# Sums of squares behind two feed-forward parts: ones times squares on TensorE between the half tiles, in place of GpSimd's adds

## The chip, the cores and the metric

The kernel runs on one core of a Trainium2 chip. The metric is device time in microseconds of one execution, taken as the median of several runs.

## The reference, cut to what matters

A model of four layers on 512 tokens of width 1024, in fp32. The change lies behind the two gated feed-forward parts of the first two layers, where this is computed (g are gain vectors, f is the feed-forward result):

```python
f = conv_glu_ffn(rms_norm(x, ffn_pre_g[layer]), ...)      # 1024 -> 2 x 2816 -> 1024
x = x + rms_norm(f, ffn_post_g[layer])                    # "m": statistic over f
# behind layer 0:
hkv = rms_norm(x, kv_norm_g); kv = hkv @ w_kv             # "x": statistic over the new x
h = rms_norm(x, mix_pre_g[1]); q = h @ w_q
# behind layer 1 (second model):
h = rmsnorm(x, norm_mix_g[0]) * (1 + sc1) + sh1
u = h @ s5_w_in                                           # then the S5 recurrence
```

So between the last product of a feed-forward part and the first product of what follows there are two RMS norms, one after the other: mean of f squared, rstd, x updated, mean of x squared, rstd, x scaled.

## The kernel before, in words

Activations lie transposed: a chunk c (0 to 7) is 128 channels on the partitions by 512 tokens. Every weight product is done in three fp32r matmuls (L470 hi by hi, L471 lo activation, L472 lo weight). For that ScalarE writes the high part of a weight tile (`split_hi`, L1114) and VectorE the low part (`split_lo`, L1843), one tile ahead of TensorE, and each normalised chunk is split in the same way (ScalarE `split_halves`, L1173; VectorE L1913 or L1915 in `norm_half`). All engines run their own instruction streams in written order and meet at semaphores; a wait at the head of a stream holds all that stands behind it.

At the two places of the change the work is cut into halves h of 256 tokens, so that half 0's norms can run beside half 1's products. I write "tile 0" and "tile 1" for the last two weight tiles of the output product (`out_pair`: tile 0 half 0, tile 1 half 0, tile 0 half 1, tile 1 half 1; 11 chunks of 3 matmuls, 33 in each), which make chunks 6 and 7 of f. Then comes the first product of the next part: behind the first feed-forward part a key tile and a value tile for half 0 (48 matmuls each), then half 1; behind the second one the two tiles of the S5 input product, also 48 each and half 0 first. A dictionary of hooks, keyed (tile, half, chunk), says at which chunk TensorE stops between its products to do something for a norm.

The norms of one half before: ScalarE squares a chunk (L1147) into one of two buffers, GpSimd adds it to sqsum (L2791), TensorE multiplies sqsum by a column of ones (`norm_sum`, L574: tokens come to lie on partitions), ScalarE takes the root (`norm_std`, L1156), VectorE the reciprocal (L1888), TensorE spreads it over all partitions (`norm_spread`, L581), and VectorE uses it: L1930 and L1934 update x chunk by chunk (`post_halves`), L1908 scales x (`norm_half`). I call the statistics m0, x0, m1, x1: of f or of the new x, for half 0 or 1.

At the start of the program the same norms are already done in another way: each squared chunk is a matmul with a full 128 x 128 matrix of ones (L589, `start_sum`), summed in PSUM. A root over one row of 256 tokens (L1280) and two matmuls with a one-column output (L598) bring it back to partitions, and the reciprocal is L2059.

The order on VectorE before, behind a feed-forward part: x of half 0 (eight chunks, with f of half 1 in between), low part of weight tile A, three chunks of half 1's x, then `norm_half(0)`, low part of weight tile B, five chunks of half 1's x, `norm_half(1)`. Tile B is the value tile, or the second S5 input tile.

## Time and profile before

| | |
|---|---|
| median of 3 runs | 2524.06 us (2520.86 to 2525.45) |
| the profiled execution: its own time | 2525.14 us |
| its span in the trace | 2523.3 us |
| TensorE busy | 94% of the span |
| VectorE, ScalarE, GpSimd busy | 57%, 42%, 18% |
| chain that ended last | TensorE 76%, VectorE 13%, ScalarE 5% |

The time is the span and 1.8 us around it. The places of the change lie at 414 to 482 us and at 1080 to 1140 us of the span. Rows of the timeline give the start, the duration, and in brackets how long the engine had been idle and who released it. Matmuls overlap in the pipeline, so a matmul's cost in a stream is the distance between starts, not its duration.

### The profile page before, as it was taken

The numbers are of one execution on the slowest core, as the hardware profiler recorded it, in microseconds if no ns is written. First come the engines' busy times: TensorE is split into PE (matmuls) and PEld (weight loads), VectorE is DVE, ScalarE is ACT, GpSimd is POOL, SyncE is SP. The second block draws the span as 40 slices with busy tenths as digits, with TensorE's granted clock in tenths as the row PEclk, the third lists the DMA queues.
The fourth block names the chain that finished last, engine by engine and source line by source line (L and its number), as shares of the span: only waits on it lengthen the run. The fifth ranks groups of instructions, "written<-read, shape, count | busy, mean of one in ns | idle before, by whom it ended". The sixth has DMA issues, their size and how long they took to land.

```text
span 2523.3 us, 34462 instructions
## 1 busy us (share of the span) xinstructions
PE 2368.9 (94%) x12994; PEld 1990.8 (79%) x12994; DVE 1429.5 (57%) x1988; ACT 1064.6 (42%) x1545; POOL 455.3 (18%) x408
## 2 busy tenths in 40 slices
PE   9999998888899999879798999999999999999998
PEld 8788877767788788667588888888877778988887
DVE  5675677857477757668735423336656642542433
ACT  5553543435545334543344313325446652431331
POOL 0230232322333223135410000011002201000001
PEclk9999999899899999979899999999999999999999
DMA  5345552212235455343121222222211202222221
GB/s 199 136 181 178 182 178 95 94 61 88 89 122 189 160 176 188 136 161 139 70 100 68 100 100 97 87 79 99 103 52 36 70 34 101 84 100 99 86 98 67
DMA packets 56346, 282.49 MB, mean 112 GB/s; under 512 B 7996, under 2 KB 19008, under 8 KB 28336
## 3 DMA queue, kind: packets, MB, share of 16 engines
q1 hardware_dynamic: 34144, 213.84, 23.6%
q0 software_dynamic: 12560, 58.80, 6.7%
q10 hardware_dynamic: 9536, 8.39, 1.0%
q8 instruction: 72, 1.18, 0.2%
q14 instruction: 34, 0.28, 0.0%
HBM read 265.14 MB, written 15.86 MB: 111 GB/s over the span
## 4 chain that ended last, share of the span: by engine, by line
PE 76%; DVE 13%; ACT 5%; issue 3%; POOL 2%; DMA 0%; ACTq 0%; DVEq 0%; SPq 0%; POOLq 0%
PE ps L470 22%; PE ps L471 21%; PE ps L472 21%; DVE w_lo L1843 3%; ACT w_hi L1114 2%; PE ps L1017 1%; PE ps L1018 1%; PE ps L1019 1%; POOL gl L2863 1%; DVE tg L1908 1%; DVE v L2484 1%; PE ps L1051 1%; POOL sqsum L2791 1%; DVE ada_w L1851 1%; PE ps L790 1%
## 5 line engine op out<-in xcount | busy, mean ns | idle before, releaser
L470 PE MATMUL ps<-h_hi,w_hi 128*128 128x512 f32 (+1 forms) x2016 | 743.3, 369 | 35.0 <-DVE w_lo L1843 21.1
L471 PE MATMUL ps<-h_lo,w_hi 128*128 128x512 f32 (+1 forms) x2016 | 732.6, 363 | 0.0
L472 PE MATMUL ps<-h_hi,w_lo 128*128 128x512 f32 (+1 forms) x2016 | 732.0, 363 | 0.0
L1843 DVE TENSOR_TENSOR w_lo<-raw,w_hi 128x2048 fp32r<-128x2048 f32 x193 | 442.1, 2291 | 463.1 <-ACT w_hi L1114 462.9
L1114 ACT ACTIVATE w_hi<-raw 128x2048 fp32r<-128x2048 f32 x193 | 369.0, 1912 | 391.5 <-PE ps L472 389.2
L470 PEld LDWEIGHTS ps<-h_hi,w_hi 128*128 128x128 f32 x2016 | 387.7, 192 | 102.0 <-issue 19.7
L470 PE MATMUL ps<-a_hi,w_hi 128*128 128x512 f32 (+1 forms) x1164 | 428.6, 368 | 30.4 <-DVE f L2300 13.7
L471 PEld LDWEIGHTS ps<-h_lo,w_hi 128*128 128x128 f32 x2016 | 388.2, 193 | 57.7 <-issue 1.0
L472 PEld LDWEIGHTS ps<-h_hi,w_lo 128*128 128x128 f32 x2016 | 388.1, 192 | 57.5
L471 PE MATMUL ps<-a_lo,w_hi 128*128 128x512 f32 (+1 forms) x1164 | 424.9, 365 | 0.0
L472 PE MATMUL ps<-a_hi,w_lo 128*128 128x512 f32 (+1 forms) x1164 | 424.8, 365 | 0.0
L2791 POOL TENSOR_TENSOR sqsum<-sqsum,sq 128x256 f32<-128x256 f32 (+1 forms) x124 | 122.7, 990 | 1029.2 <-issue 604.8
L470 PEld LDWEIGHTS ps<-a_hi,w_hi 128*128 128x128 f32 x1164 | 223.8, 192 | 70.1 <-DVE a_lo L2287 9.3
L472 PEld LDWEIGHTS ps<-a_hi,w_lo 128*128 128x128 f32 x1164 | 223.7, 192 | 34.2
L471 PEld LDWEIGHTS ps<-a_lo,w_hi 128*128 128x128 f32 x1164 | 224.1, 193 | 33.7
L2863 POOL TENSOR_TENSOR gl<-gl,tv 128x512 f32<-128x512 f32 x44 | 119.7, 2721 | 220.0 <-ACT gl L1350 220.0
L1147 ACT ACTIVATE sq<-x 128x256 f32<-128x256 f32 (+1 forms) x88 | 41.3, 475 | 240.1 <-DVE x L2556 96.1
L1851 DVE SCALAR_TENSOR_TENSOR ada_w<-ada_w,cond 128x1024 f32<-128x1024 f32 x96 | 113.4, 1218 | 0.0
L2278 DVE SCALAR_TENSOR_TENSOR tg<-ps,vec,tg 128x511 f32<-128x511 f32 x88 | 65.5, 744 | 42.8 <-ACT tg L1345 40.3
L1352 ACT ACTIVATE a_hi<-gl 128x512 f32 (+1 forms) x44 | 27.8, 632 | 132.9 <-POOL gl L2863 132.9
L2287 DVE TENSOR_TENSOR a_lo<-gl,a_hi 128x512 f32 (+1 forms) x44 | 30.5, 692 | 90.5 <-ACT a_hi L1352 90.5
L2836 POOL DMA_DIRECT2D ada_w<-ada_dram x47 | 27.6, 587 | 252.9 <-DVE ada_w L1851 247.5
(397 smaller groups left out, 2716.3 us busy)
## 6 DMA issues: line engine op xcount, KB each, us to landing
raw<-weights_dram SPq DMA_DIRECT2D x161, 1024.0 KB, 4.8
ada_w<-ada_dram POOLq DMA_DIRECT2D x48, 1024.0 KB, 5.1
raw<-weights_dram SPq DMA_DIRECT2D x32, 704.0 KB, 4.0
par<-par_dram SPq DMA_DIRECT2D x8, 1152.0 KB, 7.9
par_dram<-plane POOLq DMA_DIRECT2D x10, 512.0 KB, 3.9
tab<-tab_dram SPq DMA_DIRECT2D x8, 512.0 KB, 5.7
x_tok<-x_rows_dram SPq DMA_DIRECT2D x4, 512.0 KB, 5.8
x<-x_in_dram SPq DMA_DIRECT2D x1, 2048.0 KB, 14.2
```

The costliest lines, as they stand in the source:

```text
L470: nc.tensor.matmul(dst, w_hi[:, o:o + P], rhs_hi, start=start, stop=False)
L471: nc.tensor.matmul(dst, w_hi[:, o:o + P], rhs_lo, start=False, stop=False)
L472: return nc.tensor.matmul(dst, w_lo[:, o:o + P], rhs_hi, start=False, stop=last)
L1114: nc.scalar.activation(w_hi[:, u * TILE:(u + 1) * TILE], raw[:, u * TILE:(u + 1) * TILE], ACT.Copy).then_inc(w_hi_done, 1)
L1147: nc.scalar.activation(dst, src, ACT.Square, **scaled).then_inc(sq_ready, 1)
L1352: nc.scalar.activation(chunk(a_hi, slot.now()), chunk(gl, u), ACT.Copy).then_inc(a_hi_done, 1)
L1843: nc.vector.tensor_tensor(w_lo[:, o], raw[:, o], w_hi[:, o].bitcast(f32), SUB).then_inc(w_split, 1)
L1851: ins = nc.vector.scalar_tensor_tensor(w, w, 1.0, cond[:, :], MUL, MUL, accum_out=mod_at[:, m:m + 1])
L2278: ins = nc.vector.scalar_tensor_tensor(t[:, u * T + s:(u + 1) * T], ps[:, (2 * u + m) * T:(2 * u + m) * T + T - s], v("conv_w", j + (wcol ...
L2287: nc.vector.tensor_tensor(chunk(a_lo, slot.now()), chunk(gl, u), chunk(a_hi, slot.now()).bitcast(f32), SUB).then_inc(a_ready, 1)
L2791: gp.tensor_tensor(dst, dst, src, ADD).then_inc(sq_added, 1)
L2863: gp.tensor_tensor(chunk(gl, u), chunk(gl, u), chunk(tv, u), MUL).then_inc(prod_done, 1)
```

## The change

Behind both feed-forward parts the statistics are summed as at the start: ScalarE squares a half chunk into one of four slots of sq, and TensorE multiplies it by the matrix of ones into a bank of PSUM. GpSimd still adds the first six chunks of f, which come as whole tiles; TensorE takes its two halves in as one product each (`pooled_sum`). The roots, columns and reciprocals are those of the start. The hooks put these products between the chunks of the half tiles. On ScalarE and VectorE the order is changed too. "f" names the place behind the first feed-forward part, "g" the one behind the second. The helpers of the start are renamed and shared (`start_sum` is `square_sum`, `start_col` is `std_column`, `start_rstd` is `rstd_column`), with one list of slots for all squares; the start does the same work in the same order.

TensorE:

```diff
+        def square_sum(name):
+
+            norm, c = name[:-1], int(name[-1])
+            b0, col = SUM_AT[norm]
+            pe.wait_ge(sem("start_act"), STEP[name])
+            s = SLOT[name]
+            nc.tensor.matmul(bank(b0, TH, off=col), ones[:, :], sq[:, s * TH:(s + 1) * TH], start=(c == 0), stop=(c == DC - 1)).then_inc(sem("start_pe"), 1)
+
+        def pooled_sum(p, h):
+
+            pe.wait_ge(sq_added, POOLED[p])
+            b0, col = SUM_AT[f"{p}m{h}"]
+            nc.tensor.matmul(bank(b0, TH, off=col), ones[:, :], halved(sqsum, 0, h), start=True, stop=False)
+
+        def std_column(norm):
+
+            b0, col = COL_AT[norm]
+            pe.wait_ge(std_done, C["std"].after())
             for b in range(2):
-                last = nc.tensor.matmul(bank(b0, 1, off=col + b), rstd[0:1, h * TH + b * P:h * TH + (b + 1) * P], ident[0:1, 0:1], start=True, stop=True)
+                last = nc.tensor.matmul(bank(b0, 1, off=col + b), std_row(norm)[:, b * P:(b + 1) * P], ident[0:1, 0:1], start=True, stop=True)
             last.then_inc(sem("start_pe"), 1)
...
-        def second_norm():
-
-            sum_of[1]()
+        def second_norm(p):
+
+            square_sum(p + "x07")
+            std_column(p + "x0")
+            spread_of[0]()
+
+        def last_column(norm, *rest):
+
+            for name in rest:
+                square_sum(name)
+            std_column(norm)
             spread_of[1]()
-            sum_of[0]()
-            spread_of[0]()
...
+        def out_hooks(p):
+
+            return {(1, 0, 8): lambda: (pooled_sum(p, 0), square_sum(p + "m06")), (0, 1, 3): sums(p + "m07"), (0, 1, 5): column(p + "m0"),
+                    (0, 1, 7): spread_of[0], (1, 1, 1): sums(p + "x00"), (1, 1, 2): sums(p + "x01"), (1, 1, 3): sums(p + "x02"),
+                    (1, 1, 5): sums(p + "x03"), (1, 1, 6): sums(p + "x04"), (1, 1, 7): sums(p + "x05"), (1, 1, 9): sums(p + "x06")}
+
+        def mixed_hooks(p):
+
+            return {(0, 0, 2): lambda: (pooled_sum(p, 1), square_sum(p + "m16")), (0, 0, 3): sums(p + "m17"), (0, 0, 6): column(p + "m1")}
+
+        def second_hooks(p):
+
+            return {**mixed_hooks(p), (1, 0, 0): spread_of[1], (1, 0, 2): sums(p + "x10"), (1, 0, 3): sums(p + "x11"), (1, 0, 4): sums(p + "x12"),
+                    (1, 0, 5): sums(p + "x13", p + "x14"), (1, 0, 6): sums(p + "x15"), (1, 0, 7): sums(p + "x16"),
+                    (0, 1, 0): lambda: last_column(p + "x1", p + "x17")}
...
-            out_pair(f"ffn{layer}_out_b", FH, 1, a_hi, a_lo, {(0, 1, 7): sum_of[0], (1, 1, 3): spread_of[0]})
-            second_norm()
+            out_pair(f"ffn{layer}_out_b", FH, 1, a_hi, a_lo, out_hooks("fg"[layer]))
+            second_norm("fg"[layer])
...
-                if n == 1 and h == 0:
-                    sum_of[1]()
                 for k in range(DC):
+                    if (n, k) in VALUE:
+                        VALUE[n, k]()
...
+        VALUE = {(0, 0): spread_of[1], **{(0, c + 4): sums(f"fx1{c}") for c in range(4)}, **{(1, c - 4): sums(f"fx1{c}") for c in range(4, 8)},
+                 (1, 5): column("fx1"), (1, 7): spread_of[1]}
```

ScalarE:

```diff
+        def dense_square(name, src, **scaled):
+
+            if name in BEFORE:
+                act.wait_ge(sem("start_pe"), STEP[BEFORE[name] + "_sum"])
+            s = SLOT[name]
+            start_step(name, nc.scalar.activation(sq[:, s * TH:(s + 1) * TH], src, ACT.Square, **scaled))
+
+        def dense_std(norm, eps):
+
+            b0, col = SUM_AT[norm]
+            act.wait_ge(sem("start_pe"), STEP[norm + "7_sum"])
+            nc.scalar.activation(std_row(norm), bank(b0, TH, 0, 1, off=col), ACT.Sqrt, bias=eps).then_inc(std_done, 1)
+
+        def second_norm(f_half, eps, dst, p, shift=None):
+
+            def x_dense(h, *chunks):
+                for c in chunks:
+                    act.wait_ge(x_ready, C["x"].after())
+                    dense_square(f"{p}x{h}{c}", halved(x, c, h))
+
+            act.wait_ge(sq_added, C["sq"].n)
             f_half(0, 0)
             f_half(1, 0)
-            norm_std(EPS_A, 0)
-            x_halves(0, 0, 1, 2)
+            dense_std(p + "m0", EPS_A)
+            x_dense(0, 0, 1)
+            split_hi()
+            x_dense(0, *range(2, DC))
             f_half(0, 1)
-            x_halves(0, 3, 4)
+            dense_std(p + "x0", eps)
             f_half(1, 1)
-            x_halves(0, 5)
-            norm_std(EPS_A, 1)
-            x_halves(0, 6, 7)
+            split_halves(0, range(5), dst, shift)
+            dense_std(p + "m1", EPS_A)
             split_hi()
-            norm_std(eps, 0)
-            x_halves(1, 0, 1, 2)
-            split_halves(0, range(DC), dst, shift)
-            split_hi()
-            x_halves(1, 3, 4, 5, 6, 7)
-            norm_std(eps, 1)
+            split_halves(0, range(5, DC), dst, shift)
+            x_dense(1, *range(DC))
+            dense_std(p + "x1", eps)
             split_halves(1, range(DC), dst, shift)
             g.after(2)
```

VectorE and GpSimd:

```diff
+        def second_norm(f_half, post, gains, dst_hi, dst_lo, p, shift=None):
 
             f_half(0, 0)
             f_half(1, 0)
-            rstd_of(0)
+            rstd_column(p + "m0")
             rstd_on_all()
             post_halves(0, (0, 1, 2), post)
             f_half(0, 1)
-            post_halves(0, (3, 4), post)
+            post_halves(0, range(3, DC), post)
+            split_lo()
+            rstd_column(p + "x0")
             f_half(1, 1)
-            post_halves(0, (5, 6, 7), post)
-            rstd_of(1)
+            rstd_on_all()
+            norm_half(0, gains, dst_hi, dst_lo, shift, {7: lambda: rstd_column(p + "m1")})
             split_lo()
             rstd_on_all()
-            post_halves(1, (0, 1), post)
-            rstd_of(0)
-            post_halves(1, (2,), post)
-            rstd_on_all()
-            norm_half(0, gains, dst_hi, dst_lo, shift)
-            split_lo()
-            post_halves(1, (3, 4, 5, 6, 7), post)
-            rstd_of(1)
+            post_halves(1, range(DC), post)
+            rstd_column(p + "x1")
             rstd_on_all()
             norm_half(1, gains, dst_hi, dst_lo, shift)
             g.after(2)
...
-        def second_adds(f_first, then=None):
+        def first_adds(p):
 
             zero(C["norm"].n)
+            add_chunks(6)
```

TensorE, behind the first feed-forward part, between the last product of tile 1 half 1 (ending in L472, or L492 in the changed file) and the first key product. Before:

```order
L472 MATMUL ps<-a_hi,w_lo 128x256
L574 MATMUL ps<-ones,sqsum 128x1 x2
L581 MATMUL ps<-ident,rcol 128x128 x2
L574 MATMUL ps<-ones,sqsum 128x1 x2
L581 MATMUL ps<-ident,rcol 128x128 x2
L470 MATMUL ps<-a_hi,w_hi 128x256
```

After, where L612 is a square's sum, L625 the column and L602 the spread:

```order
L490 MATMUL ps<-a_hi,w_hi 128x256
L491 MATMUL ps<-a_lo,w_hi 128x256
L492 MATMUL ps<-a_hi,w_lo 128x256
L612 MATMUL ps<-sq,ones 128x256
L625 MATMUL ps<-ident,sq 128x1 x2
L602 MATMUL ps<-ident,rcol 128x128 x2
L490 MATMUL ps<-a_hi,w_hi 128x256
```

The sum and spread of m1 are gone from this place (they now stand within the key and before the value product), and x0's one sum is its eighth; seven more stand among tile 1 half 1's products.

TensorE, behind the second feed-forward part, at the end of the second S5 input tile's half 0, after:

```order
L490 MATMUL ps<-h_hi,w_hi 128x256
L491 MATMUL ps<-h_lo,w_hi 128x256
L492 MATMUL ps<-h_hi,w_lo 128x256
L612 MATMUL ps<-sq,ones 128x256
L625 MATMUL ps<-ident,sq 128x1 x2
L602 MATMUL ps<-ident,rcol 128x128 x2
L490 MATMUL ps<-h_hi,w_hi 128x256
```

Before, L574 stood 12 matmuls ahead of this place and only L581 stood in it; now the last square's sum, the column and the spread follow each other here.

ScalarE, behind the first feed-forward part, from the squares of x of half 0 to those of half 1. Before:

```order
L1156 ACTIVATE rcol<-ps 128x2
L1147 ACTIVATE sq<-x 128x256 x2
L1114 ACTIVATE w_hi<-raw 128x2048
L1156 ACTIVATE rcol<-ps 128x2
L1147 ACTIVATE sq<-x 128x256 x3
L1173 ACTIVATE a_hi<-tg 128x256 x8
L1114 ACTIVATE w_hi<-raw 128x2048
L1147 ACTIVATE sq<-x 128x256 x5
```

After:

```order
L1234 ACTIVATE sq<-x 128x256 x2
L1163 ACTIVATE w_hi<-raw 128x2048
L1234 ACTIVATE sq<-x 128x256 x6
L1234 ACTIVATE sq<-f 128x256
L1240 ACTIVATE sq<-ps 1x256
L1234 ACTIVATE sq<-f 128x256
L1222 ACTIVATE a_hi<-tg 128x256 x5
L1240 ACTIVATE sq<-ps 1x256
L1163 ACTIVATE w_hi<-raw 128x2048
L1222 ACTIVATE a_hi<-tg 128x256 x3
L1234 ACTIVATE sq<-x 128x256 x8
```

Both weight splits have moved: tile A's stands among the squares of half 0, and tile B's, behind the root of m1, between the fifth and the sixth high part.

## Rows read from the trace of the kernel before

**Rows 1.** Busy time per engine, the page's section 1: us, share, instructions.

```profile
PE 2368.9 (94%) x12994; PEld 1990.8 (79%) x12994; DVE 1429.5 (57%) x1988; ACT 1064.6 (42%) x1545; POOL 455.3 (18%) x408
```

**Rows 2.** Waits of TensorE over the whole span: us, times, longest.

```profile
PE ps L574 <- POOL sqsum L2791: 27.6, 12, 5.0
```

**Rows 3.** Timeline of TensorE, first feed-forward part's end: start us, duration us, instruction.

```profile
420.14 0.36 PE L470 MATMUL ps<-a_hi,w_hi 128*128 128x256 f32 x1 [1.99 <-DVE f L2300]
...
430.01 0.36 PE L470 MATMUL ps<-a_hi,w_hi 128*128 128x256 f32 x1
...
432.84 0.28 PE L472 MATMUL ps<-a_hi,w_lo 128*128 128x256 f32 x1
438.09 1.01 PE L574 MATMUL ps<-ones,sqsum 128*128 128x1 f32 x4 [4.97 <-POOL sqsum L2791]
...
448.65 0.55 PE L470 MATMUL ps<-a_hi,w_hi 128*128 128x256 f32 x1 [1.79 <-DVE a_lo L1913]
```

**Rows 4.** Timeline of TensorE, the same place, second half.

```profile
469.61 0.39 PE L470 MATMUL ps<-a_hi,w_hi 128*128 128x256 f32 x1 [1.69 <-DVE a_lo L1913]
```

**Rows 5.** Timeline of TensorE in the first feed-forward part's opening, sums between products.

```profile
46.71 0.60 PE L589 MATMUL ps<-sq,ones 128*128 128x256 f32 x2
...
47.86 0.38 PE L589 MATMUL ps<-sq,ones 128*128 128x256 f32 x1
```

**Rows 6.** Timeline of all engines at the opening: from a last sum to products.

```profile
35.97 1.13 PE L589 MATMUL ps<-sq,ones 128*128 128x256 f32 x4 [0.21 <-ACT sq L1265]
37.14 0.37 ACT L1280 ACTIVATE rstd<-ps 1x256 f32<-1x256 f32 x1 [0.92 <-PE ps L589]
37.42 1.89 ACT L1114 ACTIVATE w_hi<-raw 128x2048 fp32r<-128x2048 f32 x1
...
39.18 1.27 DVE L1908 SCALAR_TENSOR_TENSOR tg<-x,vec,ps 128x256 f32<-128x256 f32 x3 [0.80 <-PE ps L581]
...
40.92 0.38 PE L470 MATMUL ps<-h_hi,w_hi 128*128 128x256 f32 x1 [1.78 <-DVE h_lo L1913]
```

**Rows 7.** Timeline of VectorE at the opening, no GpSimd work beside it.

```profile
54.50 0.87 DVE L1930 SCALAR_TENSOR_TENSOR f<-f,vec,ps 128x256 f32<-128x256 f32 x2 [1.17 <-PE ps L581]
...
59.65 0.75 DVE L1934 TENSOR_TENSOR x<-x,f 128x256 f32<-128x256 f32 x2
```

**Rows 8.** Timeline of ScalarE at the opening, squares of x.

```profile
60.10 0.75 ACT L1265 ACTIVATE sq<-x 128x256 f32<-128x256 f32 x2 [0.31 <-DVE x L1934]
```

**Rows 9.** Timeline of VectorE behind the first feed-forward part.

```profile
430.29 0.87 DVE L1930 SCALAR_TENSOR_TENSOR f<-f,vec,ps 128x256 f32<-128x256 f32 x2 [2.69 <-PE ps L581]
...
437.77 1.42 DVE L1934 TENSOR_TENSOR x<-x,f 128x256 f32<-128x256 f32 x2
...
454.09 2.29 DVE L1843 TENSOR_TENSOR w_lo<-raw,w_hi 128x2048 fp32r<-128x2048 f32 x1 [1.28 <-ACT w_hi L1114]
```

**Rows 10.** Timeline of ScalarE behind the first feed-forward part.

```profile
425.26 1.28 ACT L1156 ACT_TABLE_LOAD   x1
```

**Rows 11.** Timeline of TensorE behind the second feed-forward part, first half.

```profile
1080.46 0.55 PE L470 MATMUL ps<-a_hi,w_hi 128*128 128x256 f32 x1 [4.05 <-DVE f L2300]
...
1111.54 0.55 PE L470 MATMUL ps<-h_hi,w_hi 128*128 128x256 f32 x1 [1.84 <-DVE h_lo L1915]
```

**Rows 12.** Timeline of TensorE, the same place, second half.

```profile
1131.20 0.39 PE L470 MATMUL ps<-h_hi,w_hi 128*128 128x256 f32 x1 [1.75 <-DVE h_lo L1915]
```

**Rows 13.** Timeline of ScalarE behind the second feed-forward part.

```profile
1086.89 0.92 ACT L1147 ACTIVATE sq<-f 128x256 f32<-128x256 f32 x2 [3.64 <-DVE f L2332]
```

**Rows 14.** Timeline of VectorE behind the second feed-forward part.

```profile
1117.32 2.29 DVE L1843 TENSOR_TENSOR w_lo<-raw,w_hi 128x2048 fp32r<-128x2048 f32 x1 [1.19 <-ACT w_hi L1114]
```

**Rows 15.** Stretches: us, busy per engine, granted clock (PEclk), DMA share, GB/s.

```profile
41.00:46.00 5.00, 5.00 (x25) 4.71 (x25) 3.63 (x11) 3.01 (x10) 0.00 (x0) 0.66 0.11 46
67.00:72.00 5.00, 4.79 (x39) 4.79 (x40) 4.47 (x13) 3.43 (x7) 0.00 (x0) 1.00 0.00 0
449.00:454.00 5.00, 5.00 (x25) 5.00 (x25) 3.81 (x11) 3.76 (x6) 0.00 (x0) 0.50 0.00 0
```

151 lines of the change are left out of this document (65 added, 86 removed).

## The prediction

> **What bounds the kernel now.** I read the busy times first: TensorE is busy 94% of the span, no other engine over 57% [rows 1]. So a change pays only where TensorE stands still. The list of its waits comes next: waits for GpSimd's adds are the largest entry, 27.6 us in 12 waits [rows 2], six of them at the two changed places. There I read the timeline. Behind the first feed-forward part the last output product starts at 432.84, then come 5 us of waiting for an add, two short sums and spreads, and key products only at 448.65: a hole of 15.7 us [rows 3]. The second half's key products start at 469.61 [rows 4]. Behind the second feed-forward part the same two points are 1111.54 and 1131.20 [rows 11, 12]. What counts is how these four starts move; between them TensorE must also do the new work.
>
> **Prices.** A sum among products: one start to the next in the opening is 1.15 us with six products between, which cost 0.12 each (24 from 430.01 to 432.84), so 0.43 [rows 3, 5]. A boundary gets 3 + 8 + 3 + 8 = 22 of them, 9.5 us of TensorE, where four groups of one-column sums go, which cost it little. From a last sum to a scaled x I use the opening: two sums start at 35.97, the second at about 36.35; the root at 37.14, VectorE's first scaling at 39.18, products at 40.92: 0.8, 2.8 and 4.6 after the last sum [rows 6]. A column is a part of the 2.0 from root to scaling; I take 0.5 for it in a stream. Eight chunks of x: VectorE starts at 54.50, ScalarE squares the seventh at 60.10 and has the eighth at 60.85, 0.73 a chunk and 6.35 in all [rows 7, 8]. A weight split is 1.9 on ScalarE and 2.3 on VectorE [rows 6, 9].
>
> GpSimd's adds also slow VectorE: two x updates take 1.42 beside them and 0.75 alone [rows 7, 9]. So I cost all updates at the opening's pace. The Trainium skill ("GPSIMD Engine Reference", Specifications) says the two share their SBUF interfaces, with contention for VectorE instructions with two SBUF inputs; the trace agrees by these two rows. Without it, the sum would be about 1 us worse at each place.
>
> **First place, half 0.** Tile 1 half 0 starts at 420.14 [rows 3]. 24 products, two sums (their inputs are ready), 9 products: 425.0. m0's last square is ready at 426.1 and summed by 426.6. ScalarE loads a table behind its square as now, 1.28 [rows 10], so the root ends at 427.8 and the column waits 0.4; spread at 429.1, VectorE at 429.75 instead of 430.29 [rows 9]. Tile 0 half 1 now ends at 430.9. Tile 1 half 1 has 33 products (4.0) and seven sums (3.0), waits 0.2 for the first square and 1.3 for the third, since ScalarE does weight split A ahead of it (432.1 to 434.0). Its end, and so x0's last sum, is 439.4: TensorE is the limit, the squares are ready by 436.5. Add 2.8: VectorE scales from 442.2; add 4.6: key products at 444.0, **4.6 us earlier** than 448.65 [rows 3].
>
> Most of this is then given back on ScalarE. Its order is five high parts, root of m1, weight split B, three high parts. The root needs m1's last sum, which follows three chunks of key products (2.2) and two sums: 447.05. Root 447.8 to 448.2, split B to 450.05, the sixth high part to 450.45; VectorE's low part and the sixth chunk of key products at 451.1, two us after TensorE has run dry. VectorE stands in m1's reciprocal until the column behind that chunk, then does two low parts (to 453.3) and its part of split B to 455.5. The value product waits for that: 455.8. Before, split B was at 454.09 to 456.38 [rows 9] and the value product at 456.9. **1.1 us of the 4.6 are left.**
>
> **First place, half 1.** Before, three of eight chunks of x were done by then; now all eight follow: spread, VectorE from 456.5, the last square ready 6.35 later, 462.8. TensorE has 48 products (5.8), eight sums (3.4), column and spread (0.9) and a 0.5 wait for the first square; the root is hidden behind products. Spread at 466.2, VectorE at 466.85, products at 468.5 instead of 469.61 [rows 4]: **-1.1 us**. GpSimd's last add no longer has to be waited for; that pays for the three chunks.
>
> **Second place, half 0.** The pattern is the same with two differences. Tile 1 half 0 starts at 1080.46 at the slower clock, and the square of chunk 6 is only ready at 1087.3, because VectorE is late: square from 1086.89 [rows 11, 13]. m0's first square sum stands in tile 1 half 0, eight chunks in, at about 1086.0, and waits 1.3 us that cost nothing before. By the same steps m0's spread is at 1093.0, tile 1 half 1 ends at 1103.35, products start at 1107.95, **3.6 us earlier** than 1111.54 [rows 11]. Then the same chain on ScalarE (with shift 0.79 a chunk): last sum of m1 at 1111.1, split B on ScalarE to 1114.05, on VectorE to 1119.75. Before it ended at 1117.32 + 2.29 = 1119.61 [rows 14]. The second S5 input tile starts at 1119.95: **+0.1 us**.
>
> **Second place, half 1.** Here nothing hides the tail. TensorE does the spread (0.4), waits 0.5 for x's first square, does 48 products (5.8) and seven sums (3.0): 1129.65. Then come x1's last sum, root, column and spread with no product between them (the order shown with the change), 4.6 us: 1134.2 instead of 1131.20 [rows 12], **+3.0 us**. Before, the sum stood 12 products earlier and root and reciprocal ran behind these. After this place TensorE's next products only wait for x, and the S5 loop starts from them, so I let the whole shift through.
>
> **The clock.** Behind the opening's own hole of this kind (3.8 us, ending at 40.92) the granted clock is 0.66 on average over 41 to 46 us, so about 3.4 us of it at half, 1.2 GHz; that takes 1.7 us of work from TensorE. Behind the 15.7 us hole it is half for all of 449 to 454. Behind the opening's second hole, of the same shape, it is full from 67 to 72 [rows 15]. The new holes (440 to 444, 1103.8 to 1108) are like these two, so a slow stretch is about one in two, and one ahead of m1's last sum moves everything behind it. I take one for both places together, +1.7 us; the bounds are none (0) and two in each place (+7). The Trainium skill ("TensorE: Matmul & The Clock Gate", What's actually happening) says the moment of a clock change isn't tied to the program's start, so that one kernel can show different numbers of slow matmuls; one execution can't show that. By that rule the 1.7 would be a spread and not a shift.
>
> **Sum.** -1.1 + 3.0 + 1.7 = +3.6 us. The profiled execution is 2525.14 (span 2523.3 and 1.8 around it), which gives 2528.7; it lies 1.1 above the median of the runs shown, so on the median's scale I predict **2527.7 us**. A measurement of this kernel can tell about 0.2%, 5 us, from no change, so this counts as the same.
>
> **Rivals.**
> - *Both places lose* (0.24): m1's sum, root, split B chain is caught by slow stretches at both places, and the dense second halves too, which have no slack for them. That is more than one stretch at each place, up to four times 1.7: -1.1 + 3.0 + 3.4 to 6.8, or +5.3 to +8.7, around 2531. For it: half clock behind the long hole and behind one of the opening's; against it: TensorE idles less in all than before.
> - *It ends even* (0.16): no slow stretch, and x1's last sum at the second place finds TensorE ahead of me by a microsecond or two, since sums and products overlap better than in the opening: then x1's tail loses only what it must: -1 to +1, 2524.
> - *It is faster* (0.10): the 4.6 and 3.6 us of the first halves are kept. That needs m1's last sum to land before ScalarE is through its fifth high part (446.0; I have 447.05), or split B to lie ahead of the need; the value product would then be bound by TensorE, from 452 instead of 455.8. Decided at 1 us earlier. That alone is -3.5 at each place against my sum; with the second place's +3.0 as it is, -1.1 + 3.0 - 7 = -5, 2519. For it: VectorE is free of GpSimd here; against it: split B's 1.9 us stand in ScalarE's order whatever comes early.
> - *The forecast's case* (0.50): +1.5 to +5, 2525.5 to 2529, whose likeliest is the sum.
>
> The range 2521 to 2532 holds the forecast's case, the even one and most of the first rival. Faster by over 0.2% 0.10, within it 0.64 (forecast and even, less the forecast's upper end), slower 0.26.
>
> **What would show it.** Key products 23.9 us behind the start of tile 1 half 0 (28.5 before); a TensorE wait of about 2 us at the sixth chunk of the key tile, released through ScalarE's split; the value tile starting 35.7 us behind the same point; at the second place products 27.5 us behind the start of tile 1 half 0 (31.1 before), and in half 1 53.7 (50.7 before), with sum, root, column and spread alone on the chain for 4.6 us. Waits of TensorE for GpSimd fall by the six. I am wrong if the key tile runs without that wait, if a sum in the stream costs clearly less than 0.43, or if the S5 loop starts no later for products that do.

## The result, and the profile after

The changed kernel takes 2530.64 us in the median (2526.66 to 2535.89, 12 runs), against 2524.8 for the kernel before on the same chip (12 runs): ratio 1.0028, 95% interval 1.0021 to 1.0036. It is 5.3 to 9.1 us slower, a little more than the 0.2% that can be told from no change. The forecast was 2527.7 us and "the same", with a range of 2521 to 2532.

The profiled execution of the changed kernel took 2535.24 us, one of the longest of its 12, 4.6 above the median. The page's row of busy times:

```profile
PE 2389.5 (94%) x13082; PEld 2007.4 (79%) x13082; DVE 1423.2 (56%) x1988; ACT 1064.6 (42%) x1545; POOL 424.9 (17%) x364
```

TensorE is still busy 94% [rows 1]. Its list of waits (what it waited for, us in all, times, longest):

```profile
PE ps L490 <- DVE w_lo L1904: 20.1, 11, 4.9
...
PE ps L594 <- POOL sqsum L2848: 11.9, 6, 3.3
PE ps L490 <- DVE h_lo L1976: 10.8, 10, 3.5
```

The change did what it says: waits for GpSimd are down from 27.6 us in 12 to 11.9 in 6 [rows 2]. The time did not follow. TensorE's timeline, first place (to 471.91) and second place; the rows answer to [rows 3, 4] and [rows 11, 12]:

```profile
419.59 0.36 PE L490 MATMUL ps<-a_hi,w_hi 128*128 128x256 f32 x1 [2.41 <-DVE f L2357]
...
435.30 0.48 PE L612 MATMUL ps<-sq,ones 128*128 128x256 f32 x1 [1.00 <-ACT sq L1234]
...
440.39 0.59 PE L612 MATMUL ps<-sq,ones 128*128 128x256 f32 x2
441.45 0.60 PE L625 MATMUL ps<-ident,sq 1*128 1x1 f32 x4 [0.46 <-ACT sq L1240]
442.32 0.71 PE L602 MATMUL ps<-ident,rcol 128*128 128x128 f32 x4 [0.26 <-DVE rcol L2003]
444.81 0.55 PE L490 MATMUL ps<-a_hi,w_hi 128*128 128x256 f32 x1 [1.78 <-DVE a_lo L1974]
...
450.50 0.82 PE L612 MATMUL ps<-sq,ones 128*128 128x256 f32 x2
...
454.35 0.39 PE L490 MATMUL ps<-a_hi,w_hi 128*128 128x256 f32 x1 [1.61 <-DVE a_lo L1974]
...
458.98 0.49 PE L602 MATMUL ps<-ident,rcol 128*128 128x128 f32 x2 [0.84 <-DVE w_lo L1904]
...
471.91 0.39 PE L490 MATMUL ps<-a_hi,w_hi 128*128 128x256 f32 x1 [1.34 <-DVE a_lo L1974]
...
1080.65 0.55 PE L490 MATMUL ps<-a_hi,w_hi 128*128 128x256 f32 x1 [4.06 <-DVE f L2357]
...
1085.88 0.59 PE L618 MATMUL ps<-sqsum,ones 128*128 128x256 f32 x2
1088.91 0.93 PE L612 MATMUL ps<-sq,ones 128*128 128x256 f32 x2 [2.44 <-ACT sq L1234]
...
1110.53 0.55 PE L490 MATMUL ps<-h_hi,w_hi 128*128 128x256 f32 x1 [1.85 <-DVE h_lo L1976]
...
1120.16 0.39 PE L490 MATMUL ps<-h_hi,w_hi 128*128 128x256 f32 x1 [1.76 <-DVE h_lo L1976]
...
1124.91 0.71 PE L602 MATMUL ps<-ident,rcol 128*128 128x128 f32 x4 [0.90 <-DVE w_lo L1904]
...
1134.76 0.60 PE L612 MATMUL ps<-sq,ones 128*128 128x256 f32 x2
1135.82 0.60 PE L625 MATMUL ps<-ident,sq 1*128 1x1 f32 x4 [0.46 <-ACT sq L1240]
1136.68 0.71 PE L602 MATMUL ps<-ident,rcol 128*128 128x128 f32 x4 [0.26 <-DVE rcol L2003]
1139.15 0.39 PE L490 MATMUL ps<-h_hi,w_hi 128*128 128x256 f32 x1 [1.75 <-DVE h_lo L1976]
```

Tile 1 half 0 starts at 419.59 at the first place and at 1080.65 at the second. Half 0's products come 25.2 and 29.9 us behind it (28.5 and 31.1 before): the hole is indeed shorter. But half 1's products come 52.3 and 58.5 us behind it (49.5 and 50.7 before). The two losses, 2.8 and 7.8, are 10.6 us, and this execution is 10.1 above the profiled one of before. So in this execution the two places hold the whole difference, and it arises behind the first products.

Why so late? The windows over the first key products (busy time of each engine, then PEclk):

```profile
444.00:446.00 2.00, 1.19 (x5) 1.22 (x6) 2.00 (x6) 1.38 (x4) 0.00 (x0) 0.53 0.00 0
446.00:448.00 2.00, 2.00 (x11) 1.91 (x10) 1.97 (x6) 0.24 (x1) 0.00 (x0) 0.50 0.00 0
448.00:450.00 2.00, 2.00 (x8) 1.73 (x7) 0.00 (x0) 0.00 (x0) 0.00 (x0) 0.50 0.03 8
450.00:452.00 2.00, 2.00 (x14) 1.88 (x13) 0.00 (x0) 0.64 (x2) 0.00 (x0) 0.76 0.00 0
```

(PEclk is the third figure from the end.) TensorE is at its lower level, 1.2 GHz, for almost 7 us behind the hole, and m1's last sum comes at 450.50 instead of the forecast 447.05; 0.8 us of that was lost before the first product. In the same windows VectorE and ScalarE run dry: everything waits for that sum. ScalarE's timeline has it as a wait of 5.12 us ahead of m1's root:

```profile
451.36 0.37 ACT L1240 ACTIVATE sq<-ps 1x256 f32<-1x256 f32 x1 [5.12 <-PE ps L612]
```

At the second place there is one wait more. VectorE's and ScalarE's timelines:

```profile
1087.94 0.42 DVE L2389 TENSOR_TENSOR f<-f,ps 128x256 f32<-128x256 f32 x1 [7.07 <-DMA tab_dram<-tv]
```

```profile
1088.44 0.42 ACT L1234 ACTIVATE sq<-f 128x256 f32<-128x256 f32 x1 [5.01 <-DVE f L2389]
```

VectorE stands 7.07 us until a table for the S5 part is stored to DRAM, then makes chunk 6 of f; ScalarE squares it, and TensorE, whose order now has that square's sum inside tile 1 half 0, waits 2.44 us. The kernel before has the same wait of VectorE, but 5.75 us long in its profile. Of the other profiles here, that of the second place alone has 5.63 us; ten have 6.9 to 7.1, the first place alone among them, whose order here is the old one; and in the last (before, split B early) VectorE waits for TensorE and no longer for the store. So the store lands early or late against TensorE's work, and the order of the sums does not decide which.

### The profile page after: what moved, and what is told of

It is laid out like the page before. It is cut to its first block, busy times and chain, and to the rows that moved or that the text cites. A ratio compares the mean times of both kernels' runs of the same rounds, so it can differ in the third digit from the quotient of the medians.

```text
span 2533.6 us, 34562 instructions
## 1 busy us (share of the span) xinstructions
PE 2389.5 (94%) x13082; PEld 2007.4 (79%) x13082; DVE 1423.2 (56%) x1988; ACT 1064.6 (42%) x1545; POOL 424.9 (17%) x364
## 4 chain that ended last, share of the span: by engine, by line
PE 76%; DVE 13%; ACT 5%; issue 3%; POOL 2%; DMA 1%; ACTq 0%; DVEq 0%; SPq 0%; POOLq 0%
PE ps L490 21%; PE ps L491 21%; PE ps L492 21%; DVE w_lo L1904 3%; ACT w_hi L1163 2%; PE ps L1066 1%; PE ps L612 1%; PE ps L1068 1%; PE ps L1067 1%; POOL gl L2905 1%; DVE v L2541 1%; PE ps L1100 1%; DVE tg L1969 1%; DVE ada_w L1912 1%; PE ps L839 1%
## 5 line engine op out<-in xcount | busy, mean ns | idle before, releaser
L492 PE MATMUL ps<-h_hi,w_lo 128*128 128x512 f32 (+1 forms) x2016 | 733.0, 364 | 0.0
L490 PE MATMUL ps<-a_hi,w_hi 128*128 128x512 f32 (+1 forms) x1164 | 433.2, 372 | 33.0 <-DVE f L2357 14.4
L492 PEld LDWEIGHTS ps<-h_hi,w_lo 128*128 128x128 f32 x2016 | 389.0, 193 | 57.0
L492 PE MATMUL ps<-a_hi,w_lo 128*128 128x512 f32 (+1 forms) x1164 | 425.3, 365 | 0.0
L2848 POOL TENSOR_TENSOR sqsum<-sqsum,sq 128x256 f32<-128x256 f32 (+1 forms) x84 | 93.4, 1112 | 978.0 <-issue 595.9
L492 PEld LDWEIGHTS ps<-a_hi,w_lo 128*128 128x128 f32 x1164 | 224.4, 193 | 34.0
L1196 ACT ACTIVATE sq<-x 128x256 f32<-128x256 f32 (+1 forms) x56 | 28.4, 508 | 209.4 <-DVE x L2613 96.1
L2879 POOL DMA_DIRECT2D ada_w<-ada_dram x47 | 27.6, 588 | 253.0 <-DVE ada_w L1912 247.6
## 6 DMA issues: line engine op xcount, KB each, us to landing
x<-x_in_dram SPq DMA_DIRECT2D x1, 2048.0 KB, 14.4
```

Source lines behind the costliest of these rows:

```text
L490: nc.tensor.matmul(dst, w_hi[:, o:o + P], rhs_hi, start=start, stop=False)
L492: return nc.tensor.matmul(dst, w_lo[:, o:o + P], rhs_hi, start=False, stop=last)
L1196: nc.scalar.activation(dst, src, ACT.Square, **scaled).then_inc(sq_ready, 1)
L2848: gp.tensor_tensor(dst, dst, src, ADD).then_inc(sq_added, 1)
```

## The experiments

The measure in each profile is the pair of distances from the start of tile 1 half 0 to half 1's first products of the next stage. The time is the median; the last column the profiled execution's own.

| kernel | first | second | sum | median us | ratio to before | profiled us |
|---|---|---|---|---|---|---|
| before | 49.5 | 50.7 | 100.2 | 2523 to 2525 | | 2525.1 |
| after | 52.3 | 58.5 | 110.8 | 2530.6 | 1.0028 | 2535.2 |
| first place alone | 49.8 | 50.8 | 100.6 | 2523.0 | 0.9996 | 2523.9 |
| second place alone | 49.5 | 54.8 | 104.3 | 2529.3 | 1.0022 | 2530.3 |
| fillers | 48.9 | 56.4 | 105.3 | 2529.9 | 1.0025 | 2529.9 |
| split B late | 50.5 | 56.3 | 106.8 | 2526.6 | 1.0009 | 2529.5 |
| m0's square late | 50.9 | 55.9 | 106.8 | 2530.1 | 1.0024 | 2526.2 |
| m1 in the hole | 47.1 | 53.1 | 100.2 | 2525.5 | 1.0014 | 2525.2 |
| both of these | 47.3 | 50.4 | 97.7 | 2524.2 | 1.0003 | 2524.1 |
| and x1 pulled forward | 47.3 | 49.6 | 96.9 | 2521.8 | 0.9992 | 2522.4 |
| and split B early | 43.5 | 48.6 | 92.1 | 2515.9 | 0.9962 | 2516.5 |
| first place of that alone | 44.9 | 50.6 | 95.5 | 2513.7 | 0.9959 | 2512.3 |
| thin sums (less work) | 49.9 | 57.1 | 107.0 | 2530.1 | 1.0022 | 2530.2 |
| before, split B early | 48.1 | 48.0 | 96.0 | 2520.6 | 0.9988 | 2522.2 |

Outside the two places the spans of twelve of these profiles lie within 4 us (2421.0 to 2424.7); that of "m0's square late" is 2417.7 and that of "first place of that alone" 2415.0. So the sum orders the kernels only roughly.

One thing hides in the first column. In five profiles (after, split B late, m1 in the hole, first place of that alone, before with split B early) tile 1 half 0 of the first place begins behind a wait of 2.4 us and runs 3.4 us of its time at half clock; in the other nine that wait is 1.99 us and the clock stays full. It costs 1.4 us: with the same order, "and split B early" has 43.5 without it and "first place of that alone" 44.9 with it. The changed kernel's 2.8 us of loss at the first place hold these 1.4.

**The first place alone.** Second place as before (its old orders on all engines are put back; only the list of squares is shown).

```diff
-SQUARES = ... + BOUNDARY["f"] + BOUNDARY["g"]
+SQUARES = ... + BOUNDARY["f"]
```

> The change at the first place (behind feed-forward part 0) alone, the second as before. My theory (the loss is what the chain m1's sum, root, weight split B and the bare tail of x1 cost, plus slow clock stretches): first place -1 us at full clock and about +3 with a slow stretch ahead of m1's last sum, so -1 to +3 us against the kernel before, about +1 (ratio 1.000 to 1.001). Rival (the 22 sums a place are simply more work for TensorE than the holes give back): both places cost alike, +2.9 us.

Measured 2523.04, ratio 0.9996 [0.9986, 1.0006]. The first place moves the time by -3.5 to +1.5 us, which fits the -1.1 forecast for it. Key products start 23.85 us behind tile 1 half 0 (forecast 23.9), and the sixth chunk waits 1.60.

**The second place alone.**

```diff
-SQUARES = ... + BOUNDARY["f"] + BOUNDARY["g"]
+SQUARES = ... + BOUNDARY["g"]
```

> The change at the second place alone, the first as before. My theory: this place carries most of the loss, +3 us at full clock and up to +8 with slow stretches and a longer wait for m0's first square, about +5 (ratio 1.002). Rival (plain work, alike at both places): +2.9 us. The two single places should add up to the changed kernel's +5.8.

Measured 2529.33, ratio 1.0022 [1.0013, 1.0032]: the loss of 3.3 to 8 us is here. The rival of both expectations, the sums as plain work that costs 2.9 us at either place, lies outside both intervals. The two places add up to 1.0018, the changed kernel has 1.0028 [1.0021, 1.0036]; the intervals allow that they simply add. S5 products start 27.4 us behind tile 1 half 0 (forecast 27.5). This profile is the mild case of the second place: m0's wait is 1.14 us in place of 2.44, and the half clock behind the hole lasts 3.4 us in place of 6.8.

**Fillers in the hole.** Six products with ones into an unused bank, two ahead of x0's column and four behind its spread.

```diff
             square_sum(p + "x07")
+            filler(2)
             std_column(p + "x0")
             spread_of[0]()
+            filler(4)
```

> The changed kernel with six more products of ones into an unused bank at each place, two while TensorE waits for x0's root and four behind x0's spread, so that it works through most of the 4 us hole before the first product of the next part. Results are not touched. If the slow clock is what the hole costs, the products behind it (0.21 us apart in the profile) come at full clock and the kernel gets 1.5 to 3.5 us faster than the changed one, about 2527.5. If the clock change comes whatever TensorE does for these 2.6 us, or doesn't matter, the time stays at 2530.6, or grows by up to 0.5 us a place where the filler delays the column.

Measured 2529.87, ratio 1.0025 [1.0015, 1.0035]: no gain that can be told. Its windows show one reason:

```profile
446.00:448.00 2.00, 0.79 (x7) 0.59 (x5) 0.09 (x1) 2.00 (x3) 0.00 (x0) 1.00 0.00 0
448.00:450.00 2.00, 1.50 (x10) 1.28 (x10) 0.41 (x2) 0.49 (x2) 0.00 (x0) 1.00 0.00 0
450.00:452.00 2.00, 1.52 (x8) 1.52 (x9) 2.00 (x4) 0.00 (x0) 0.00 (x0) 0.70 0.00 0
452.00:454.00 2.00, 2.00 (x11) 1.84 (x10) 0.96 (x1) 0.00 (x0) 0.00 (x0) 0.50 0.00 0
```

The clock is full behind the hole, but the wait at the sixth chunk (448.39, again 1.60) is still there, and the lower level now comes behind that one. The sixth chunk starts 30.9 us behind tile 1 half 0, where I had 31.0: at full clock the forecast's chain on ScalarE is right to 0.1 us.

This profile also gives the clock's price in rows. First products and sixth chunk at the first place, with fillers:

```profile
441.69 0.36 PE L490 MATMUL ps<-a_hi,w_hi 128*128 128x256 f32 x1
...
448.39 0.38 PE L490 MATMUL ps<-a_hi,w_hi 128*128 128x256 f32 x1 [1.60 <-DVE a_lo L1981]
```

And with the first place alone:

```profile
443.31 0.55 PE L490 MATMUL ps<-a_hi,w_hi 128*128 128x256 f32 x1 [1.78 <-DVE a_lo L2012]
...
451.43 0.38 PE L490 MATMUL ps<-a_hi,w_hi 128*128 128x256 f32 x1 [1.60 <-DVE a_lo L2012]
```

The order of work between them is the same in both. With no half clock it takes 6.7 us (6.9 at the second place); with 3.4 us of it 8.1 here, and 8.2 to 8.5 in two more profiles; with 6.8 us of it 9.4 to 9.7 at five holes. So one stretch costs 1.4 to 1.6 us at a place and a double one 2.5 to 2.9, and the second tile starts later by about as much.

**Split B behind all high parts.**

```diff
-            split_halves(0, range(5), dst, shift)
+            split_halves(0, range(DC), dst, shift)
             dense_std(p + "m1", EPS_A)
             split_hi()
-            split_halves(0, range(5, DC), dst, shift)
```

> The changed kernel with ScalarE's order at both places: all eight high parts of x, then the root of m1, then weight split B (before: five, root, split B, three). My theory: the sixth high part no longer waits for m1's sum and the 1.9 us split, TensorE's gap of about 1.7 us ahead of the sixth chunk closes and the tile after it starts 1.5 to 2.7 us earlier at each place: 3 to 5 us faster than the changed kernel, 2526 to 2527.5. Rival (plain work of the sums): no change, 2530.6, since the tile behind is bound by the sums and split B is not earlier.

Measured 2526.55, ratio 1.0009 [1.0000, 1.0018]. The sixth-chunk wait is gone (0.58 is left, a chunk later), and 4 us with it, as expected: that wait is paid in full. The rows say the same, and the clock has no part in it, since both profiles have 6.8 us of half clock behind each hole. From first products to the value product it is now 12.3 us (442.49 to 454.79), where the changed kernel has 14.2 (444.81 to 458.98); 12.4 and 14.4 at the second place:

```profile
442.49 0.55 PE L490 MATMUL ps<-a_hi,w_hi 128*128 128x256 f32 x1 [1.78 <-DVE a_lo L1973]
...
454.79 0.71 PE L602 MATMUL ps<-ident,rcol 128*128 128x128 f32 x4 [0.84 <-DVE w_lo L1903]
```

**m0's first square read two chunks of products later at the second place.**

```diff
-            return {(1, 0, 8): lambda: (pooled_sum(p, 0), square_sum(p + "m06")), ...
+            return {((1, 0, 8) if p == "f" else (0, 1, 2)): lambda: (pooled_sum(p, 0), square_sum(p + "m06")), ...
```

> One sum is moved, at the second place alone: TensorE reads m0's pooled sum and its first square (which in the changed kernel waited 2.4 us for ScalarE, behind a VectorE step that waited 7.1 us for a DMA store) two chunks later in the products, behind chunk 1 of the next half instead of ahead of it. Theory A (the second place pays for that wait, in time and in a half clock behind it): the wait of 2.4 us is gone, m0's column comes at most 0.5 us later relative to the products around it, and the kernel is 1.3 to 3 us faster than the changed one, about 2528.5 us. Theory B (the wait is hidden: what TensorE loses there it would lose at the next root anyway, because m0's statistic has 10 us to spare and the second norm's own chain sets the end): no change, 2530 to 2531 us. A wait that is seen to fall with the time unchanged says B.

Measured 2530.12, ratio 1.0024 [1.0012, 1.0035]. The 2.44 us wait and the half clock behind it are gone, and the S5 products start 27.1 us behind tile 1 half 0, not 29.9. But half of the wait only moved: TensorE now stands 1.24 us for chunk 6 of f at the start of the next half tile:

```profile
1082.57 0.38 PE L490 MATMUL ps<-a_hi,w_hi 128*128 128x256 f32 x1 [1.24 <-DVE f L2389]
```

The first place alone, with the old order here, waits 1.27 us at the same product. So with a late store TensorE waits over 1 us in either order, and only the rest comes from the sum's early place. The time moves by less than can be told, and the profile shows the lower level behind the hole and again later. By itself this run leaves A and B open; the pair below says more, by its rows.

**m1's sums in the hole.**

```diff
             square_sum(p + "x07")
+            pooled_sum(p, 1)
             std_column(p + "x0")
+            square_sum(p + "m16")
             spread_of[0]()
+            square_sum(p + "m17")
...
-            return {(0, 0, 2): lambda: (pooled_sum(p, 1), square_sum(p + "m16")), (0, 0, 3): sums(p + "m17"), (0, 0, 6): column(p + "m1")}
+            return {(0, 0, 3): column(p + "m1"), (0, 0, 6): spread_of[1]}
...
-            split_halves(0, range(5), dst, shift)
+            split_halves(0, range(2), dst, shift)
             dense_std(p + "m1", EPS_A)
+            split_halves(0, range(2, DC), dst, shift)
             split_hi()
-            split_halves(0, range(5, DC), dst, shift)
```

On VectorE m1's reciprocal comes behind chunk 5 and two x chunks ahead of split B's low part.

> At both places m1's pooled sum and its two squares' sums are read by TensorE between x0's last sum, its column and its spread, where it stands idle for about 4 us, instead of between the first products of the next stage; m1's root then comes behind the second high part on ScalarE, all of split B runs behind the eighth high part, and VectorE takes m1's reciprocal behind chunk 5. Theory A (the changed kernel loses at the first chunks of the next stage: the sums of m1 in the stream, the root between the high parts, and the gap at the sixth chunk): three sums of 0.43 us leave the stream, the gap of 1.6 to 1.8 us goes, and the value tile and the second input tile come 3 to 4 us sooner each; 5 to 8 us faster than the changed kernel, 2522.5 to 2525.5 us, so equal to the kernel before or 2 us better. Theory B (the end is set by x1's chain on VectorE and TensorE, which only the number of sums in the stream moves): 1 to 2.6 us faster, 2528 to 2529.5 us.

Measured 2525.48, ratio 1.0014 [1.0004, 1.0023]: 3.5 us (by the ratios) to 5.2 us (by the medians) faster than the changed kernel, at A's low end or between A and B. Two things are seen. The windows behind the hole:

```profile
444.00:446.00 2.00, 0.89 (x7) 0.92 (x8) 2.00 (x7) 1.67 (x5) 0.00 (x0) 1.00 0.00 0
446.00:448.00 2.00, 2.00 (x18) 1.85 (x16) 1.14 (x4) 0.83 (x2) 0.00 (x0) 1.00 0.00 0
448.00:450.00 2.00, 1.93 (x15) 1.73 (x15) 1.95 (x7) 1.06 (x3) 0.00 (x0) 1.00 0.03 8
```

No half clock. And a new wait, 2.42 us (2.41 at the second place) for split B's low part at the second tile, which took back part of what A had promised.

**Both edits together.**

> The two edits together: m1's sums in the hole at both places, and m0's pooled sum and first square two chunks later at the second place. If the two act on different waits, the gains add: 1.3 to 3 us beside the first edit alone, 2520.5 to 2523.5 us. If the wait at the second place is hidden, it reads as the first edit alone.

Measured 2524.21, ratio 1.0003 [0.9994, 1.0012], 1.3 us under the one above by the medians and 2.7 us less at the second place by the rows (50.4 against 53.1). By the medians that is the low end of "the gains add", but the two intervals overlap, so only the rows show that m0's wait was worth something: 1.0 us less of waiting (1.37 for 2.37) and no half clock behind it.

**x1's sums pulled forward** at the second place.

```diff
-            return {**mixed_hooks(p), (1, 0, 2): sums(p + "x10"), ..., (0, 1, 0): lambda: last_column(p + "x1", p + "x17")}
+            return {**mixed_hooks(p), (1, 0, 1): sums(p + "x10", p + "x11"), (1, 0, 2): sums(p + "x12"), (1, 0, 3): sums(p + "x13", p + "x14"),
+                    (1, 0, 4): sums(p + "x15"), (1, 0, 5): sums(p + "x16", p + "x17"), (1, 0, 7): column(p + "x1"), (0, 1, 0): spread_of[1]}
```

> The kernel of both edits, and at the second place x1's sums are read as early as VectorE and ScalarE deliver them (from chunk 1 of the second input tile on), with x1's column behind chunk 7 and its spread ahead of the next stage's first products, so that no root is left bare at the end. Theory A (the second place's half 1 loses the eight sums in the stream and a bare root, column and spread at its end, about 2.9 us): the bare part goes, 2 to 3 us faster than both edits without it, 2518 to 2521.5 us, 3 to 6 us faster than the kernel before. Theory B (x1's squares come so late that the sums wait in the stream): TensorE shows waits of 1 us and more at x1's sums or its column, and the time stays at that of both edits, 2521 to 2524 us. Theory C (nothing in the order matters here, and the dense sums alone cost what the changed kernel loses): 2529 us and more.

Measured 2521.79, ratio 0.9992 [0.9981, 1.0003]. This and the run above can't be told apart by their intervals; the rows can. No wait at x1's sums, so not B, and the root is covered; but second tile to half 1's products shrinks only from 13.2 to 12.4 us. The bare tail was worth 0.85 us by the rows, not 2 to 3. TensorE's timeline shows what was left, first and second place:

```profile
455.14 0.48 PE L772 MATMUL ps<-w_hi,a_hi 128*128 128x256 f32 x1 [2.40 <-DVE w_lo L1906]
...
1115.68 0.39 PE L490 MATMUL ps<-h_hi,w_hi 128*128 128x256 f32 x1 [2.42 <-DVE w_lo L1906]
```

**Split B in the hole.**

```diff
             dense_std(p + "x0", eps)
+            split_hi()
             f_half(1, 1)
...
             split_halves(0, range(2, DC), dst, shift)
-            split_hi()
```

VectorE makes the low part right behind `norm_half(0)`.

> The previous kernel (m1's sums in the hole, m0's first square later at the second place, x1's sums and column pulled forward) waits 2.4 us on TensorE at both places for split B's low part, because ScalarE makes the high part of split B (1.9 us) only behind the eighth high part and VectorE does two x chunks ahead of the low part. Here ScalarE makes split B right behind x0's root, while TensorE stands idle, and VectorE makes the low part right behind half 0's norm, where it waited 0.9 us for m1's spread. Theory A (TensorE's stream sets the end of each boundary and every wait in it counts): the wait of 2.4 us falls to under 0.5 us at both places, nothing new comes in, and the kernel is 3 to 5 us faster, 2517 to 2519.5 us. Theory B (x1's chain on VectorE sets the end): VectorE's total work is the same and only its idle 0.9 us is filled, so 1 to 2 us, 2520 to 2521.5 us, and a wait of TensorE at x1's sums, column or spread grows instead.

Measured 2515.93 (5 runs), ratio 0.9962 [0.9948, 0.9976]: 9.6 us faster than before [6 to 13] and 5.9 under the last one, more than A gave. ScalarE's timeline at the first place:

```profile
439.46 1.89 ACT L1165 ACTIVATE w_hi<-raw 128x2048 fp32r<-128x2048 f32 x1
...
441.83 0.81 ACT L1224 ACTIVATE a_hi<-tg 128x256 fp32r<-128x256 f32 x2 [0.17 <-DVE tg L1971]
```

The 1.89 us fit between the root and the first high part; only one square stands between. TensorE's rows:

```profile
443.06 0.36 PE L490 MATMUL ps<-a_hi,w_hi 128*128 128x256 f32 x1 [0.65 <-DVE a_lo L1976]
...
462.59 0.39 PE L490 MATMUL ps<-a_hi,w_hi 128*128 128x256 f32 x1 [1.34 <-DVE a_lo L1976]
```

24.0 and 43.5 us behind tile 1 half 0 (419.10), with no wait at the second tile and PEclk 1.00 in every window from 441 to 465. At the second place the distances are 27.3 and 48.6; there a wait of 0.59 us at one of x1's sums is new.

**The first place of that alone,** the second as before.

> The change at the first place alone, with m1's sums in the hole and split B early; the second place as in the kernel before. The first place alone, as the change made it, measured 0.9996 of the kernel before. If the places do not touch each other, the edits at the first place are worth about half of what both edits gave at both places together (5 us) and half of what the early split gives: 2.5 to 4 us faster than that, 2519.5 to 2521 us, ratio 0.9980 to 0.9988. If the first place had nothing left to lose (its value products cover the tail), it stays at 0.9996, 2523 us.

Measured 2513.72 (5 runs), ratio 0.9959 [0.9946, 0.9973]: faster than I expected by 6 us. Its own rows explain 4.6 us at the first place and nothing at the second. The rest, over 5 us, lies outside both places: in its profile 3.4 us ahead of the first place and 3.1 behind the second, where the kernel does the same work as before. I can't name its cause. It also means that the medians don't show a gain from the second place: with it the kernel is no faster (0.9962 against 0.9959), although the rows there are 2.1 us shorter than before.

**Thin sums.** One column in place of 256 for seven of x1's sums at the second place.

```diff
+            if norm == "gx1" and c < DC - 1:
+                nc.tensor.matmul(bank(b0, 1, off=col), ones[:, :], sq[:, s * TH:s * TH + 1], start=True, stop=True)...
```

> The changed kernel, but at the second place the first seven of x1's eight sums are products of one column in place of 256 (x1's statistic is then wrong: it is the eighth square alone); their waits and places stay. Theory A (half 1 of the second place loses the length of the sums in the stream): seven sums of 0.43 us less at most 0.1 us each leave it, 2.3 to 2.8 us faster than the changed kernel, about 2528 us. Theory B (x1's squares, their last sum and the bare root, column and spread set the end, and the stream only waits for them): under 0.5 us, 2530 to 2531 us, and a wait ahead of the last sum appears.

Measured 2530.13, ratio 1.0022 [1.0013, 1.0031]; the difference to the changed kernel is too small for the interval. TensorE's rows, with six products (0.12 each) from 1125.98 on between the first two, and six more to 1127.60:

```profile
1125.74 0.38 PE L613 MATMUL ps<-sq,ones 128*128 128x1 f32 x2 [0.33 <-ACT sq L1237]
...
1126.78 0.28 PE L613 MATMUL ps<-sq,ones 128*128 128x1 f32 x2
...
1127.72 0.28 PE L613 MATMUL ps<-sq,ones 128*128 128x1 f32 x2
```

0.94 us from sum to sum, where the changed kernel has 1.14 (1128.62 to 1129.76): so 0.22 of a sum's 0.42 us stay with a single column. Seven times 0.2 is 1.4, and from spread to column it is 9.46 us instead of 10.91. No wait took its place, so by the rows the tail is bound by TensorE's stream (A), at half of A's price.

**Before, with split B early.** Is it the split alone?

```diff
             norm_std(eps, 0)
+            split_hi()
             x_halves(1, 0, 1, 2)
             split_halves(0, range(DC), dst, shift)
-            split_hi()
```

> The kernel before, with split B's high part on ScalarE right behind x0's root (where ScalarE stood idle for 2.6 us) and not behind the eighth high part; the dense sums are not in it. It tells whether the 8 to 10 us of the two last kernels come from the early split alone. Theory A (they come from the dense sums being read where TensorE stands idle, with the early split as the last piece, and the kernel before cannot have them): VectorE's wait of 1.28 us for split B goes at both places, x1's chunks and GpSimd's adds come that much sooner, TensorE's waits ahead of x1's sums (2.44 and 1.38 us) shrink by it, and nothing at the second tile changes, since TensorE does not wait there: 1 to 2.6 us faster than the kernel before, 2521.5 to 2523 us. Theory B (the early split is worth the most of it in any order): 5 us faster and more, 2519 us or less.

Measured 2520.57, ratio 0.9988 [0.9979, 0.9997]: 3 us [0.8 to 5.3], A's order of size. TensorE's waits ahead of x1's sums shrink to

```profile
462.53 0.27 PE L574 MATMUL ps<-ones,sqsum 128*128 128x1 f32 x1 [1.44 <-POOL sqsum L2791]
...
1121.88 0.27 PE L574 MATMUL ps<-ones,sqsum 128*128 128x1 f32 x1 [0.50 <-POOL sqsum L2791]
```

from 2.44 and 1.38. The interval of the kernel with dense sums and early split ends at 0.9976, below this one's 0.9979, so neither the early split alone nor the dense sums without it (0.9992) reach the 8 to 10 us; both parts are needed. The margin is narrow, and the faster kernels have five runs each.

## Why the prediction was right in range and too low

The measured 2530.6 us lies in the range of 2521 to 2532, but above the forecast's own case (2525.5 to 2529). It is in the part that the range took from the first rival. The sums and the two chains came out; the number was saved by the width of the range, since the clock's term was too small.

**Half 0 up to the products: right.** Forecast 23.9 us, measured 23.85 with the first place alone; 27.5 at the second place, measured 27.4 with that alone. In the profile of the changed kernel it was 25.2, with the 1.4 us of half clock in tile 1 half 0, and 29.9, with m0's longer wait and the half clock behind that.

**The sum's price: right.** 0.43 forecast, 0.42 measured. The waits forecast at the third square (1.3; 1.00 measured), the sixth chunk (2; 1.61 and 1.76) and the first square of half 1 (0.5; 0.32) all appeared.

**Half 1's tail: right.** From the second tile to half 1's products I had 12.7 us at the first place and 14.2 at the second; the rows show 12.9 and 14.2. I let the second place's shift through to the S5 part, and it goes through with 1.2 us on top: TensorE's first wait for ScalarE there comes 17.5 us behind half 1's products (1156.69), 16.3 us before (1147.52). The changed kernel has a half-clock stretch in between (PEclk 0.61 and 0.54 from 1140 to 1144), which the kernel before had ahead of these products (0.64 and 0.51 from 1126 to 1130). That is outside the sum of the table, and I had it nowhere.

**m0's square at the second place: mis-sized.** Forecast 1.3 us, measured 2.44, and TensorE's windows from 1088 to 1094 read 0.81, 0.50 and 0.84 behind it, a stretch that I had nowhere. I had read the square's time from one profile, but not what it hung on: a DMA store, whose end is not fixed to TensorE's work. In the profile with the second place alone, where the store was as early as in the kernel before, that wait was 1.14, close to the forecast.

**The clock: the step that failed.** "I take one for both places together, +1.7 us", a stretch of 3.4 us. In the changed kernel's profile there is one at each place behind the hole, nearly 7 us long, besides the one just named; first products to second tile took 14.2 and 14.4 us where I had 11.8 and 12.0. That is 2.4 us at each place. The chain grows by so much because m1's last sum stands behind products that run at half clock themselves. This is the first rival's mechanism (m1's sum, root and split B caught by slow stretches), to which I gave 0.24 and 2531 us: it is nearer to the result than my forecast's case, though the first place alone does not lose.

What failed is the rate, "about one in two", taken from the opening's two holes. Six profiles (after, each place alone, split B late, m0's square late, thin sums) have ten holes of the changed form between them, and half clock follows every one: 3.4 us of it in three, 6.8 in seven. At 1.4 to 1.6 and 2.5 to 2.9 us a place that is 2.8 to 5.8 us for the two places, where I had 1.7. The price of one stretch, 1.7, was about right. The other terms (-1.1 + 3.0) and the 1.1 us by which m0's wait was too small make 3.0, which leaves 3 to 4 of the measured 6 to 7 us: within that span, or just under it (2 to 3) if the 1.2 us behind half 1's products at the second place count as well. This is a sum over single profiles; no run isolates the clock in the median.

How long the stretch is differs from execution to execution of like code, 3.4 or 6.8 us behind the same hole. It goes with the scatter: among 65 executions of the kernel before, the 14 with a mean granted clock of 0.967 or 0.968 took 2526 to 2528 us on average, the 16 with 0.971 took 2520.5 to 2521.6. The Trainium skill ("TensorE: Matmul & The Clock Gate", What's actually happening) says the moment of a clock change isn't tied to the program's start; the trace agrees as far as these differing lengths go. By that rule my 1.7 would be a spread and not a shift; the ten holes say that it is a spread on top of a shift.

What the clock alone costs in the median stays open: fillers moved the half clock instead of removing it and gained nothing that the interval can tell, and the kernels without it differ in other waits too.

**Where the gain of the shorter hole went.** Into m1's chain, through two orders. m1's sums stood in the stream behind the hole although their inputs were ready in it, and split B stood on ScalarE between high parts although ScalarE was idle in the hole. Taking split B from between the high parts gave 4 us, and with both moved into the hole the changed form is 9.6 us faster than before, 8.1 of it in the rows of the two places. My third rival ("it is faster") had named the second of these as its condition, "split B to lie ahead of the need"; what I did not see is that a hole already stood open for it.

## What to carry to other kernels

When a change shortens a hole, look at what stands in each engine's order just behind it and is already ready inside it: move that work in. Here that filled the hole, kept the clock full behind it and shortened the chain at once; dummy work did only the first two, and half clock came behind the next wait anyway. And when a sum or a square is put earlier in an order than anything read it before, follow its input back to the last DMA.

## What the runs showed of the hardware

- A product of ones with 128 x 256 fp32 squares costs 0.42 us in a stream of 0.12 us products, and still 0.22 with one column.
- Half clock (PEclk 0.50) came behind every one of ten bare holes of about 4 us, for 3.4 or 6.8 us. Much shorter waits were followed by it too, for 3.4 us: 2.4 us ahead of tile 1 half 0 in five profiles of five (1.99 us at the same product: in none of nine), 2.4 us at the second tile in two of six, and 1.6 to 1.8 us at the sixth chunk in five of ten.
- With m1's three sums in the hole, which left a longest wait of 1.13 to 1.19 us, or 0.65 to 0.71 with split B early, PEclk stayed at 1.00 for the 8 us behind it at all nine holes of the five profiles. So it did behind the two holes with fillers.
- A stretch of 3.4 us at half clock cost the chain behind the hole 1.4 to 1.6 us, and one of 6.8 us 2.5 to 2.9.
